# Two windowed-attention items scored in one visit, on four quarters of the matmul array

## The reference, cut to what matters

```python
# 8 query heads, 2 key/value heads, chunks of 64 tokens, keys: own chunk and the one before
s = jnp.einsum('bnqhgd,bnkhd->bnhgqk', q, kb) * (HEAD_DIM ** -0.5)
s = jnp.where(valid, s, NEG)
p = jax.nn.softmax(jnp.concatenate([s, sink], axis=-1), axis=-1)[..., :-1]
o = jnp.einsum('bnhgqk,bnkhd->bnqhgd', p, vb)
```

## Time and profile before

| what | value |
|---|---|
| median of 3 runs | 1875.31 us (1874.92 to 1875.57) |
| profiled execution, own time | 1874.11 us |
| its span, first to last instruction | 1872.3 us |
| PE busy | 1856.3 us, 99% of the span |
| DVE busy / ACT busy / POOL busy | 986.5 / 710.3 / 202.3 us |
| mean granted clock of PE | 0.999 of 2.4 GHz |

### The profile page before, as it was taken

One profiled execution on the slowest core, in us unless ns is written; L12 is line 12 of the kernel. 1 busy time (PEld: TensorE's weight loads), 2 busy tenths in 40 slices (PEclk: granted clock), 3 DMA queues, 4 the chain that ended last, 5 costly groups with the idle time before them and its releaser, 6 DMA issues.

```text
span 1872.3 us, 25256 instructions
## 1 busy us (share of the span) xinstructions
PE 1856.3 (99%) x9480; PEld 1534.4 (82%) x9480; DVE 986.5 (53%) x1350; ACT 710.3 (38%) x1115; POOL 202.3 (11%) x420
## 2 busy tenths in 40 slices
PE   9999999999999999999999999999999999999998
PEld 7888888888678888888888888889886888888887
DVE  6664433387757544432476544325877574444323
ACT  5333332255755333322253333223666453333321
POOL 3832000013100000000047200000130000000000
PEclk9999999999999999999999999999999999999999
DMA  6335343343223333343333443333511313333331
GB/s 197 101 103 146 95 119 93 85 144 102 57 68 91 98 93 101 95 121 94 100 93 99 108 132 113 107 95 104 161 51 53 113 57 101 93 98 114 97 93 45
DMA packets 332013, 188.61 MB, mean 101 GB/s; under 512 B 7028, under 2 KB 327512, under 8 KB 330904
## 3 DMA queue, kind: packets, MB, share of 16 engines
q1 hardware_dynamic: 325992, 168.60, 31.3%
q0 software_dynamic: 5824, 18.79, 3.3%
q10 hardware_dynamic: 112, 0.05, 0.0%
HBM read 175.72 MB, written 11.67 MB: 100 GB/s over the span
## 4 chain that ended last, share of the span: by engine, by line
PE 96%; DVE 2%; ACT 2%; issue 0%; DVEq 0%; ACTq 0%
PE ps L595 19%; PE ps L597 18%; PE ps L596 18%; PE ps L804 8%; PE ps L805 8%; PE ps L806 8%; PE ps L652 2%; PE ps L654 2%; PE ps L659 2%; PE ps L990 1%; PE ps L764 1%; PE ps L763 1%; PE ps L765 1%; PE ps L625 1%; PE ps L636 1%; PE ps L627 1%
## 5 line engine op out<-in xcount | busy, mean ns | idle before, releaser
L1677 DVE TENSOR_TENSOR wl<-raw,wh 128x1024 fp32r<-128x1024 f32 (+1 forms) x260 | 344.4, 1325 | 729.3 <-ACT wh L1175 728.0
L595 PE MATMUL ps<-xh,wh 128*128 128x512 f32 x1536 | 606.1, 395 | 2.2 <-ACT vc L1398 2.2
L597 PE MATMUL ps<-xh,wl 128*128 128x512 f32 x1536 | 598.2, 389 | 0.0
L596 PE MATMUL ps<-xl,wh 128*128 128x512 f32 x1536 | 597.9, 389 | 0.0
L1175 ACT ACTIVATE wh<-raw 128x1024 fp32r<-128x1024 f32 (+1 forms) x260 | 295.8, 1139 | 621.4 <-PE ps L806 324.6
L595 PEld LDWEIGHTS ps<-xh,wh 128*128 128x128 f32 x1536 | 288.4, 188 | 66.1 <-issue 4.8
L597 PEld LDWEIGHTS ps<-xh,wl 128*128 128x128 f32 x1536 | 288.3, 188 | 60.5
L596 PEld LDWEIGHTS ps<-xl,wh 128*128 128x128 f32 x1536 | 288.5, 188 | 60.0 <-issue 1.9
L804 PE MATMUL ps<-Hh,wh 128*128 128x512 f32 x638 | 248.4, 389 | 0.0
L806 PE MATMUL ps<-Hh,wl 128*128 128x512 f32 x638 | 248.2, 389 | 0.0
L805 PE MATMUL ps<-Hl,wh 128*128 128x512 f32 x638 | 248.2, 389 | 0.0
(11 more groups left out here) (390 smaller groups left out, 2020.0 us busy)
## 6 DMA issues: line engine op xcount, KB each, us to landing
raw<-in_ffn_gate SPq DMA_DIRECT2D x88, 512.0 KB, 3.8
raw<-in_ffn_up SPq DMA_DIRECT2D x88, 512.0 KB, 3.8
raw<-in_ffn_down SPq DMA_DIRECT2D x64, 704.0 KB, 4.5
raw<-in_w_in SPq DMA_DIRECT2D x28, 512.0 KB, 4.1
raw<-in_w_out SPq DMA_DIRECT2D x16, 512.0 KB, 3.6
xrow<-in_x SPq DMA_DIRECT2D x4, 512.0 KB, 7.2
ssm_t<-evict POOLq DMA_DIRECT2D x8, 256.0 KB, 3.6
ssm_v<-evict POOLq DMA_DIRECT2D x8, 256.0 KB, 3.5
```

Source lines behind the costliest of these rows:

```text
L595: pe.matmul(bank, w_tile(True, slot, kw), xh[:, kx, :], start=first, stop=False)
L596: pe.matmul(bank, w_tile(True, slot, kw), xl[:, kx, :], start=False, stop=False)
L597: return pe.matmul(bank, w_tile(False, slot, kw), xh[:, kx, :], start=False, stop=last)
L1677: V.tensor_tensor(w_low(slot, k0, nk), raw[:, slot4, 0:nk - k0, :], w_high(slot, k0, nk).bitcast(F32), ALU.subtract).then_inc(w_split, 1)
```

## The change

Scores of both swa items of a head pair are computed in one visit of PE. The odd item uses the other two quarters: head a reads its own input half and writes the opposite output half, in bank 3. Its probabilities therefore lie with the heads swapped, which `attend`, the sinks and their negatives (now one copy per parity) take into account. The visit waits for the exponentials of both items before. Except at step 0 it comes behind `attend` and `turn` of the even step, and a half of projection 12 comes one step earlier. On DVE, `norms(s-2)` comes ahead of `maxes(s)` in steps 2 to 7. `PAD` keeps the layout of the memory behind the larger tables of sinks.

```diff
+                    if kind == "swa":
+                        if i:
+                            return
+                        if n:
+                            pe.wait_ge(s_exp, g)
...
+                        pe.wait_ge(qk_rdy, l * (1 + SWA_PAIRS) + 2 + j)
+                        pe.matmul(ps[S_BANK[0]][:, 0:P], identb[:, :], maskb[:, P:2 * P], start=True, stop=False,
+                                  skip_group_check=True)
+                        for cc in range(ITEM_CHUNKS):
+                            for o in range(2):
+                                c = ITEM_CHUNKS * o + cc
+                                k0 = keys_from(c)
+                                for a in range(2):
+                                    r, ro = slice(64 * a, 64 * a + 64), slice(64 * (a ^ o), 64 * (a ^ o) + 64)
+                                    mm = pe.matmul(ps[S_BANK[o]][ro, cc * P:(cc + 1) * P], qa[r, j, c * CHUNK:(c + 1) * CHUNK],
+                                                   kz[r, j // 2, k0:k0 + P], start=(c > 0), stop=True, skip_group_check=True)
+                                if cc == ITEM_CHUNKS - 1:
+                                    mm.then_inc(s_mm, 1)
+                        return
...
-                                               probT[:, n % 2, cc * P + a * CHUNK:cc * P + (a + 1) * CHUNK],
+                                               probT[:, n % 2, cc * P + (a ^ i) * CHUNK:cc * P + (a ^ i) * CHUNK + CHUNK],
...
-                    if s < N_ITEMS:
+                    if s < N_ITEMS and (s == 0 or s >= N_SWA):
                         scores(s)
...
                         turn(s - LAG_T)
+                    if 0 < s < N_SWA:
+                        scores(s)
...
-                for a in range(2):
-                    r = slice(64 * a, 64 * a + 64)
-                    mine = sinkr[r, :, :].rearrange("p l (j a) -> p l j a", a=2)[:, :, :, a]
-                    link(V.tensor_copy(sinks[r, :, :], mine))
-                    link(V.tensor_scalar(nsinks[r, :, :], mine, -1.0, None, ALU.mult))
+                for o in range(2):
+                    for a in range(2):
+                        r = slice(64 * (a ^ o), 64 * (a ^ o) + 64)
+                        mine = sinkr[r, :, :].rearrange("p l (j a) -> p l j a", a=2)[:, :, :, a]
+                        link(V.tensor_copy(sinks[r, o, :, :], mine))
+                        link(V.tensor_scalar(nsinks[r, o, :, :], mine, -1.0, None, ALU.mult))
...
                 for s_ in range(N_ITEMS + LAG_N):
+                    if s_ < N_SWA and s_ >= LAG_N:
+                        norms(s_ - LAG_N)
                     if s_ < N_ITEMS:
                         maxes(s_)
-                    if s_ >= LAG_N:
+                    if s_ >= N_SWA:
                         norms(s_ - LAG_N)
...
-PART_AT = {0: (9, 0, 2), 2: (10, 0, 2), 4: (11, 0, 2), 7: (12, 0, 2), 8: (12, 2, 4), 10: (13, 0, 2), 11: (13, 2, 4),
+PART_AT = {0: (9, 0, 2), 2: (10, 0, 2), 4: (11, 0, 2), 6: (12, 0, 2), 8: (12, 2, 4), 10: (13, 0, 2), 11: (13, 2, 4),
```

More of the change, by code:

```diff
@@ L92 @@
 N_ITEMS = len(ITEMS)
+assert GROUPS_OF_CHUNKS == 2
 N_PAIRS = SWA_PAIRS + FOX_PAIRS
@@ L241, in build @@
         sinkr = sb("sinkr", [P, DEPTH, SWA_HEADS])
-        sinks = sb("sinks", [P, DEPTH, SWA_PAIRS])
-        nsinks = sb("nsinks", [P, DEPTH, SWA_PAIRS])
+        sinks = sb("sinks", [P, 2, DEPTH, SWA_PAIRS])
+        nsinks = sb("nsinks", [P, 2, DEPTH, SWA_PAIRS])
         fbias = sb("fbias", [P, DEPTH])
@@ L951, in scores @@
                     g = l * N_ITEMS + n
+                    if kind == "swa":
[3 more added lines that the diff above has]
+                            pe.wait_ge(s_exp, g)
+                        if n == 0:
+                            pe.wait_ge(vs_rdy, l + 1)
+                        pe.wait_ge(qk_rdy, l * (1 + SWA_PAIRS) + 2 + j)
[12 more added lines that the diff above has]
+                        return
                     if n >= 2:
@@ L955, in scores @@
                     bank = ps[S_BANK[n % 2]]
[L956 to L963, removed]
-                            for a in range(2):
-                                r = slice(64 * a, 64 * a + 64)
-                                mm = pe.matmul(bank[r, cc * P:(cc + 1) * P], qa[r, j, c * CHUNK:(c + 1) * CHUNK],
-                                               kz[r, j // 2, k0:k0 + P], start=(c > 0), stop=True, skip_group_check=True)
-                    else:
+                    if kind == "fox":
                         if i == 0 and h % 2 == 0:
@@ L1434, in exps @@
                                            bias=stat[:, b, cc:cc + 1], accum_out=stat[:, b, 4 + cc:5 + cc]).then_inc(act_c, 1)
-                        act.activation(stat[:, b, 8:12], stat[:, b, 0:4], ACT.Exp, bias=sinks[:, l, j:j + 1]).then_inc(s_exp, 1)
+                        act.activation(stat[:, b, 8:12], stat[:, b, 0:4], ACT.Exp, bias=sinks[:, i, l, j:j + 1]).then_inc(s_exp, 1)
                     else:
@@ L2003, in maxes @@
                                               AX.X, ALU.max, negate=True))
-                        V.tensor_scalar(stat[:, b, 0:4], stat[:, b, 0:4], nsinks[:, l, j:j + 1], None, ALU.min).then_inc(s_max, 1)
+                        V.tensor_scalar(stat[:, b, 0:4], stat[:, b, 0:4], nsinks[:, i, l, j:j + 1], None, ALU.min).then_inc(s_max, 1)
                     else:
@@ L2427 @@
 SUM_AT_K = (3, 2)
-PAD = 196
+PAD = 180
 SQUARE_AT = {6: 0, 8: 1, 10: 2, 12: 3, 17: 4, 18: 5, 21: 6}
```

## The result

| what | before | after |
|---|---|---|
| median | 1875.26 us | 1879.72 us |
| fastest execution | 1874.49 us | 1878.02 us |
| profiled execution, own time | 1874.11 us | 1880.15 us |
| its span | 1872.3 us | 1878.3 us |
| PE busy | 1856.3 us | 1853.6 us |

A forecast was written before the change was run, and what follows sets the result against it. It took PE as fully loaded, with DVE and ACT nearly level. Waits outweighing saved work cost 1.3 us per layer, 2.6 in all: 1874.11 becomes 1876.7, plus 1.2 for the median gives 1877.9 us; range 1872.5 to 1881.5.

The forecast's parts named there:

- Neither sign of being wrong: Attention stage: wrong if item 4's maximum comes before 461, or PE's waits behind it sum to under 2 us per layer.
- Steps 1 to 6: Attention stage, place by place: item 4's maximum 2.4 us later, PE 1.1 us late at item 5's attend despite saved visits.
- Step 7: GLU matmuls: input lands at 491.7, PE would be there at 491.5 and waits 0.2 us; total 1.3 us late per layer.
- The rest: Outside the place-by-place sum: normalisation order and index changes free, start-up operations hidden, up to 0.3 us if uncovered.
- The four operations on the sinks: DVE at the start: four more tiny operations, 0.2 us each, hidden, up to 0.3 us if that cover is gone.
- the last rival: A further stall, from the start-up operations or projection 12's weight part: 1 to 2 us more, 1879 to 1880 us; 8%.
- the weight part for projection 12: DVE writes it behind item 4's late maximum, until about 464, while PE wants it at about 465.6; a possible stall.
- Two quarters at a time: Score visits: each takes 0.88 us more, 1.8 us per layer, 3.6 in all, 1881.5 us; 12%.
- The faster rival: Attention stage: PE stays the bound if DVE and ACT catch up, 2.4 us saved per layer, 1870.5 us; 12%.
- Half of projection 12 in step 6: PE in step 6: moving this half there fills one gap and uncovers the attend of item 3; no separate size given.

The follow-up runs named there:

- e4: The changed kernel with seven bf16 matmuls without use placed in PE's wait for `vT`: 1877.93 us, ratio 1.0016.
- e5: e3 with PE's order in steps 4 and 6 made visit, attend, turn, then the projection part: 1870.05 us, ratio 0.9971.
- e7: The changed kernel measured again as it is: 1879.16 us, ratio 1.0021.
- e8: The kernel before with only DVE's order changed, normalisation of item n-2 ahead of the maximum of item n in steps 2 to 7: 1874.90 us.
- e11: e5 without the move of `vT` ahead of the maxima of items 0 and 1 on DVE: 1872.39 us, ratio 0.9984.
- e2: The changed kernel with the visit of items 4 and 5 first in step 4, and item 0's turn and ACT's order moved to allow it: 1880.65 us.
- e3: The changed kernel with e2's edit and, on DVE, `vT` ahead of the maxima of items 0 and 1: 1877.82 us, ratio 1.0015.
- e10: The changed kernel with the first half of projection 12 back in step 7, as in the kernel before: 1881.11 us, ratio 1.0032.
- e6: The changed kernel with the visit's two loops exchanged, so that two quarters work at a time: 1880.32 us, ratio 1.0026.
- e9: e5 with the visit's two loops exchanged, so that two quarters work at a time: 1872.18 us, ratio 0.9985.

## Why the prediction was right, and by how much it was short

**Sign and mechanism.** Right: the change saves PE's work and makes PE wait for more. The forecast was 1877.9 us and within 0.2% of before; the median is 1879.7 us, inside the range, just beyond that 0.2%, which the prediction gave 0.20; the interval of the ratio, 1.0016 to 1.0029, holds the 0.2%. Neither sign of being wrong came: the maximum of item 4 stands at 462.0 us in e4, and PE's waits behind it sum to over 3 us.

**Steps 1 to 6.** These hold to 0.25 us. I read them in e4, where the clock is out of it, less its 0.80 us ahead of the stage. PE waited for `vT` 1.34 us in the changed kernel (said: 1.1). `ssm_out` came 0.3 us later (0.2), the turn of item 0 0.7 us earlier (0.8). The maximum of item 4 came 2.43 us later (2.4), the exponentials of item 5 2.41 (2.4), the attend of item 5 1.14 (1.1). In the second layer of the changed kernel, that maximum is 7.22 us from its place in the earlier trace rows, less 4.78: 2.4 us. The 4.1 us of work saved show in e5, 4.0 and 4.2 us.

**Step 7.** The product ahead of the GLU came 1.86 us later (1.8), the layer 1.39 and 1.22 us (1.3). Here the transfer is the loose end: in the first layer of the changed kernel the GLU did not wait, in the second layer of e7 it waited 0.5 us.

**The rest, and the clock.** This is the step that was short, by two terms; how much of the median the second makes is argued and not shown. The four operations on the sinks were not hidden. Between 30.10 and 46.21 us the changed kernel falls back by 0.30 us, and all the others that have these operations by 0.26 to 0.30 us, while e8, without them, has 0.00; the prediction had "hidden, up to 0.3 if that cover is gone", and the cover was gone. And it had no term for the clock. With 0.3 for the start and 2.6 for the layers the sum is 1875.1 + 2.9 = 1878.0 us; e4, whose wait is filled, has 1877.93. The changed kernel had 1.2 to 1.8 us more than e4, and one fall of the clock at `vT` cost 1.4 us in its profile. That the falls explain the difference of the medians is supported by this and by the split of e11's executions, not shown: the intervals of the two ratios overlap, and e7, the same kernel, had its fall elsewhere, where it cost nothing. The measured time is that of the last rival, 1879 to 1880 us, but not for its cause: of its two stalls the four operations gave 0.3 us, and the weight part for projection 12 none, since no row of PE's waits has it.

**Two quarters at a time.** The rule of the Trainium skill (TensorEngine Tiling (Array Packing), Gotcha 1: row tiles cannot access one PSUM bank at once) would have made four quarters as slow as two. The rows say otherwise: 1.04 against 1.52 us for the same records, with both row halves writing in both banks. The prediction was right to set the rule aside here. But its price for this rival was wrong. It took 0.11 us a step from 1.02 us less 0.16 over 8 steps; it is 0.06, and the other 0.5 us comes once for each visit. The 0.16 us, which it called a change of tile form, is the time from the mask matmul's start to that of the scores (0.15 us from 464.22 to 464.37 in the changed kernel), which the 1.02 us do not hold. So each visit would have cost 0.5 us and not 0.88, and in this kernel 1.2 us in all and not 3.6.

**The faster rival.** It said that 1870.5 us would come if PE stayed the bound, and that the maximum of item 4 decides this. The number was good: e5 has 1870.05 us, with 2.46 and 2.96 us gained in the layers, but it took another order of PE, DVE and ACT, so in part the agreement is luck. The place was too narrow. e2 and e3 brought that maximum 2 us ahead of its place before and gained little, since the next pair's visit was late in the same way. What decides is that each visit is early: both items of a pair are given to DVE and ACT at once, in the two banks, and no new score can be made until both are read. If the visit then stands behind 2.9 us of projection, an attend and a turn, both engines run dry once in every two items. DVE showed it as one gap of 6.7 us in the changed kernel and as one of 4.3 us in e2 and e3.

**Half of projection 12 in step 6.** The prediction let it fill one gap and uncover another wait, with no net price. e10, without it, is 2 us slower by the median, but its profile puts that on the clock, for which the prediction had no term; by the waits alone the step stands.

## What to carry to other kernels

Joining two items in one visit takes away the double buffering between them: put the joint visit first in its step, with what it waits for ahead of that, and put the long filler work behind. If a place frees one engine, look for the next place of the same kind before you judge the idea: here curing one of two late visits gained nothing beyond the cure of a wait, and curing both gained 9 us. Where PE is the bound and all waits are short, a new wait of a microsecond should carry a second price in the sum, for the clock. And look at the mean clock of all executions: one profile shows one of them, here even the fastest (e2).

## What the runs showed of the hardware

- Four 64x64 quarters work side by side, both row halves in each of two PSUM banks: 32 records in 1.10 us, against 1.59 us in the order with two quarters at a time (e6).
- A visit of such small matmuls has a part of some 0.5 us that doesn't grow with its records (1.02 us for 16 records, 1.52 us for 32 at the same two quarters).
- The granted clock fell to 1.2 GHz inside these layers in 7 of the 14 profiles of the study, each time in or behind waits of PE of 0.7 to 1.9 us, alone or close together. It did not in the profiles of before, e8, e9 and e2 to e5, of which e2, e3 and e5 wait over 1 us around projection 10 too. Ahead of PE's own work a fall cost 1.4 us in the changed kernel and 1.6 and 2.8 us in e10, ahead of a wait for ACT nothing.
- The kernel before is not free of this: of its 86 executions beside the three groups, 16 had a mean granted clock of 0.998 and 1875.8 to 1877.6 us, the other 70 had 0.999 or 1.0 and 1874.3 to 1876.1 us.
